# Level products of a chunked recurrence, computed and evacuated only in the columns that are queries

## What is computed

```python
def step(S, inp):
    qc, kc, vc, gc = inp
    b = jnp.cumsum(gc, axis=2)
    inter = jnp.einsum('bhtd,bhde->bhte', qc * jnp.exp(b), S)
    rel = jnp.where(lower[None, None, :, :, None],
                    b[:, :, :, None, :] - b[:, :, None, :, :], -jnp.inf)
    scores = jnp.einsum('bhtd,bhsd,bhtsd->bhts', qc, kc, jnp.exp(rel))
    intra = jnp.einsum('bhts,bhse->bhte', scores, vc)
```

## Time and profile before

| | us |
|---|---|
| median of 3 runs | 4476.14 (4475.63 to 4477.32) |
| profiled execution, time | 4479.9 |
| profiled execution, span of the trace | 4478.1 |
| TensorE busy, matmuls | 3959.1 (88%) |
| TensorE busy, weight loads | 3156.1 (70%) |
| VectorE busy | 1820.1 (41%) |
| ScalarE busy | 1096.3 (24%) |

### The profile page before, as it was taken

One profiled execution on the slowest core, in us unless ns is written; L12 is line 12 of the kernel. 1 busy time (PEld: TensorE's weight loads), 2 busy tenths in 40 slices (PEclk: granted clock), 3 DMA queues, 4 the chain that ended last, 5 costly groups with the idle time before them and its releaser, 6 DMA issues. The chain is left out here.

```text
span 4478.1 us, 55788 instructions
## 1 busy us (share of the span) xinstructions
PE 3959.1 (88%) x23797; PEld 3156.1 (70%) x23797; DVE 1820.1 (41%) x2978; ACT 1096.3 (24%) x2013; POOL 156.8 (4%) x152
## 2 busy tenths in 40 slices
PE   5798988989579999999699999999668299999996
PEld 1454455554169999999588888888644199999995
DVE  4324346752621111111278888888932611111112
ACT  1210024532110101110334554544422001010111
POOL 0000000000000000000000000000000000000000
PEclk8899988999789999999899999999889599999998
DMA  6201100013778888885310001010032478888884
GB/s 233 89 15 55 41 0 1 1 62 108 286 224 263 262 263 262 259 256 167 93 31 28 28 27 32 16 32 19 7 149 99 130 231 261 266 260 265 260 257 166
DMA packets 521950, 616.30 MB, mean 138 GB/s; under 512 B 16076, under 2 KB 466248, under 8 KB 521065
## 3 DMA queue, kind: packets, MB, share of 16 engines
q1 hardware_dynamic: 502216, 543.33, 37.3%
q0 software_dynamic: 16448, 58.73, 5.1%
q10 hardware_dynamic: 3040, 10.68, 0.6%
HBM read 558.86 MB, written 53.84 MB: 137 GB/s over the span
## 5 line engine op out<-in xcount | busy, mean ns | idle before, releaser
L1449 PEld LDWEIGHTS moe_pgu<-step_hnT,mw_w 128*128 128x128 f32 x8192 | 1118.1, 191 | 16.5 <-issue 16.5
L1449 PE MATMUL moe_pgu<-step_hnT,mw_w 128*128 128x160 f32 x8192 | 1125.8, 300 | 3.4 <-ACT step_hnT L1489 3.4
L1513 DVE TENSOR_TENSOR moe_hT<-moe_sg,moe_pgu 128x160 f32<-128x160 f32 x256 | 82.0, 321 | 1028.2 <-PE moe_pgu L1449 971.6
L1461 PE MATMUL moe_pol<-mw_w,moe_hT 128*128 128x256 f32 x2048 | 457.5, 381 | 2.3 <-DVE moe_hT L1513 1.0
L1691 PE MATMUL rec_pz<-step_hnT,rec_w 128*128 128x256 f32 x1920 | 425.2, 381 | 10.0 <-DMA rec_w<-in_r_w_in 8.0
L1461 PEld LDWEIGHTS moe_pol<-mw_w,moe_hT 128*128 128x128 f32 x2048 | 383.2, 190 | 59.0 <-DVE moe_hT L1513 10.0
L1691 PEld LDWEIGHTS rec_pz<-step_hnT,rec_w 128*128 128x128 f32 x1920 | 362.9, 191 | 58.9 <-DMA rec_w<-in_r_w_in 8.3
L1500 ACT ACTIVATE moe_sg<-moe_pgu 128x160 f32<-128x160 f32 x256 | 77.8, 304 | 1317.6 <-PE moe_pgu L1449 1317.6
L1695 PE MATMUL rec_pz<-rec_w,step_hnT 128*128 128x256 f32 x1280 | 284.8, 381 | 15.1 <-ACT rec_zg L1766 15.1
L1695 PEld LDWEIGHTS rec_pz<-rec_w,step_hnT 128*128 128x128 f32 x1280 | 241.5, 191 | 49.7 <-ACT rec_zg L1766 17.9
L1721 PE MATMUL rec_pg<-rec_ring 128*128 128x128 f32 x1600 | 198.4, 283 | 49.8 <-DVE rec_AT L2007 18.5
(11 more groups left out here) (316 smaller groups left out, 4391.6 us busy)
## 6 DMA issues: line engine op xcount, KB each, us to landing
mw_w<-in_moe_w_gu SPq DMA_DIRECT2D x256, 1024.0 KB, 11.0
mw_w<-in_moe_w_down SPq DMA_DIRECT2D x128, 1024.0 KB, 13.7
mod_w_ring<-in_mod_w SPq DMA_DIRECT2D x24, 1024.0 KB, 14.3
mw_w<-in_mod_w SPq DMA_DIRECT2D x24, 1024.0 KB, 14.3
rec_w<-in_r_w_in SPq DMA_DIRECT2D x40, 512.0 KB, 4.0
scratch_xm<-op_x ACTq DMA_DIRECT2D x20, 512.0 KB, 2.6
scratch_xn<-op_xn POOLq DMA_DIRECT2D x20, 512.0 KB, 5.2
hin_w<-in_e_w_in SPq DMA_DIRECT2D x12, 512.0 KB, 6.8
```

The source lines that it names most:

```text
L1449: m = nc.tensor.matmul(pgu[2 * (f % 2) + part][:, :], w[:, j, k, (f % 2) * P:(f % 2 + 1) * P], ring[:, k, e % 8, :], start=(k == 0), stop= ...
L1461: m = nc.tensor.matmul(pol[q // 2][:, (q % 2) * SW:(q % 2 + 1) * SW], hT[:, k, 0:CL], w[:, 8 + q, k, :], start=(k == 0), stop=(k == KD - 1))
L1513: nc.vector.tensor_tensor(hT[:, f, :], sg[:, f % 2, :], pgu[2 * (f % 2) + 1][:, :], ALU.mult).then_inc(multiplied, 1)
```

## The change

In the level products the moving operand and the output are cut to the 64 query columns of each tile; the weights stay all 128 columns. The evacuations of the levels read and write only these 64 columns, under the mask cut the same way. INTER and both DK items stay as they are. Since L64 forward no longer writes the key columns of `rec_AT`, a memset on VectorE sets these (the key half at level 64, 10 x 64 columns) to zero once a head, before VectorE waits for that product.

```diff
+        def halves(x, h, s):
+
+            return x.rearrange("p t (s h) -> p t s h", h=h)[:, :, s, :]
...
-                    into_banks(h, (d, i), lambda o, t: nc.tensor.matmul(o, kb[:, t * P:(t + 1) * P], qb[:, t * P:(t + 1) * P],
-                                                                       start=True, stop=True))
+
+                    def mm(o, t):
+                        q = qb[:, t * P:(t + 1) * P]
+                        if i != DK:
+                            q, o = (blocks(a, ITEM_LEVEL[i])[:, :, qhalf(d), :] for a in (q, o))
+                        return nc.tensor.matmul(o, kb[:, t * P:(t + 1) * P], q, start=True, stop=True)
+                    into_banks(h, (d, i), mm)
...
-                    if d == 0 and i == L64 and h:
-                        dve.wait_ge(g_full, 3 * use(h - 1, "o") + 3)
+                    if d == 0 and i == L64:
+                        if h:
+                            dve.wait_ge(g_full, 3 * use(h - 1, "o") + 3)
+                        nc.vector.memset(halves(AT[:, :, :], 64, kh), 0.0)
...
-                            last = TT(at, src, maskf[:, 0:1, :].broadcast_to([P, nt, P]), ALU.mult)
+                            last = TT(halves(at, 64, qh), halves(src, 64, qh), halves(maskf[:, 0:1, :], 64, qh).broadcast_to([P, nt, 64]), ALU.mult)
...
-                            last = nc.vector.copy_predicated(at, maskb[:, j:j + 1, :].broadcast_to([P, nt, P]), src)
+                            m = maskb[:, j:j + 1, :]
+                            if i == DK:
+                                last = nc.vector.copy_predicated(at, m.broadcast_to([P, nt, P]), src)
+                            else:
+                                hh = ITEM_LEVEL[i]
+                                m = m.rearrange("p a (b s h) -> p a b s h", s=2, h=hh)[:, :, :, qh, :].broadcast_to([P, nt, 64 // hh, hh])
+                                at, src = (x.rearrange("p t (b s h) -> p t b s h", s=2, h=hh)[:, :, :, qh, :] for x in (at, src))
+                                last = nc.vector.copy_predicated(at, m, src)
```

## The result

| | before | after |
|---|---|---|
| median, us | 4476.73 (4475.63 to 4481.53, 4 runs) | 4514.31 (4510.44 to 4515.15, 4 runs) |
| ratio after / before | | 1.0082, 95% interval 1.007 to 1.0094 |
| profiled execution, us (span) | 4479.9 (4478.1) | 4515.15 (4513.4) |

The change makes the kernel 0.8% **slower**; the forecast was 4469.2, and the range ended at 4481. Only rival D had this sign.

The account below looks back on a forecast made before the run. TensorE was taken to bound heads 0 to 6, VectorE mostly the last. Products 0, heads 0 to 6 4.1 and last head 2.8 made 6.9 us off the 4476.1 median: 4469.2 us, wanted range 4452 to 4481.

Parts of the forecast that it names:

- rival D: Halved products let TensorE's clock fall once a direction, 2.2 us each, 31 us in all, so 4500 us; chance 0.07.
- the clock of TensorE in heads 0 to 6: The sum held no clock cost in heads 0 to 6, whose windows showed a clock of 1.00.
- Products: 0: Halved level products on TensorE keep their 112 ns matmul spacing, set by the unchanged 128-column weight load; term 0.
- Rival A: Moving columns set the spacing: 112 falls to 56 ns, 63 us in heads 0 to 6, about 4406 us; chance 0.11.
- B: Spacing falls to 108 ns (4 us), or the gate copy wait shrinks (up to 15.1 us): 4450 to 4465; chance 0.24.
- Evacuations: 0.295 us a bank: VectorE's predicated copies of a bank fall from 724 to 429 ns, two-tile banks by 147 ns; about 47 us of work.
- Rival C: Evacuations out of PSUM in short runs get no shorter; only the last head's memset is left, 4476.7 us; chance 0.10.
- The memset: New VectorE memset once a head, 0.56 to 0.7 us: covered in heads 0 to 6, 0.6 us in the last.
- Heads 0 to 6: 4.1 us gained: Shorter L16 evacuation frees bank 0 0.295 us earlier, 14 times: 4.1 us off TensorE's wait and the time.
- TensorE starts L8 that much earlier, and all after it follows: In heads 0 to 6, L8 starts 0.295 us earlier per direction and the whole saving reaches the end.
- the head end "stays": TensorE's gate copy wait, 2.2 us a head, is unchanged, since both its chains hang on the DK product.
- Last head: 2.8 us gained: VectorE's work is on the path: 3 x 0.74 + 0.45 + 0.69 less 0.6 for the memset gives 2.8 us.

Follow-up runs that it names:

- e1: Changed kernel with all products computed full again, short evacuations, mask and memset kept: 4475.42 us, ratio 0.9996 to the kernel before.
- e2: Changed kernel with predicated copies over whole banks again, products halved from head 1 on, memset and short multiplication kept: 4505.26 us, ratio 1.0065.
- e5: Changed kernel with one projection product per direction moved from before L16 to between L16 and L8, products still halved: 4486.38 us, ratio 1.0017.
- e4: Changed kernel with only the L8 product halved, the other products full, evacuations short: 4480.96 us, ratio 1.0008.
- e9: Changed kernel with only the L16 product halved, the other products full, evacuations short: 4476.95 us, ratio 0.9999.
- e10: Changed kernel with only L16 and L8 halved, L64 and L32 full, evacuations short: 4509.4 us, ratio 1.0066.
- e7: Changed kernel with full products, a projection per direction moved before L8 and two last projections moved ahead of gate and norm: 4472.46 us, ratio 0.999.
- e3: Changed kernel with L64, L32 and L16 halved, the L8 product full, evacuations short: 4476.64 us, ratio 0.9998.
- e11: Changed kernel with full products, short evacuations and four added VectorE memsets ahead of the L16 evacuation, lengthening TensorE's pause: 4533.56 us, ratio 1.0124.

## Why the prediction was wrong

**The step that failed** is a term that the sum put at nothing: the clock of TensorE in heads 0 to 6. The sum has 4.1 us gained there and no price for the clock; the reason given is the sentence against rival D, answered below. The runs showed, in its place, 35.5 us for L8 and DK at the low clock and 8.5 for head ends, and with full products (e1) the 35.5 are gone.

**Products: 0. Right.** At the upper clock forty halved matmuls take 4.70 us like forty full ones (e2), and twenty take 2.34 for 2.40 us: the difference of 0.06 is the latency of the last, 219 for 275 ns, not the spacing, (2.34 - 0.22)/19 = 112 ns. Nor does the spacing shrink at the lower clock (4.50 us for twenty halved in e5's last head, 4.61 for full ones). That it is the load of 128 weight columns which keeps the pace is argued from the rows; no run changes the number of weight columns. The Trainium skill ("TensorE: Matmul & The Clock Gate", LDWEIGHTS) gives P/1.2 ns, an estimate of 107; the spacing of 112 is near it. Its isolated gap of N/2.4 + 2.5 ns (Back-to-back issue gap), by which halved products would have been worth some 60 us, does not hold here. Rival A falls, and B with it: the spacing stays at 112 ns, and the wait for the gate copy at 2.1 to 2.2 us a head.

**Evacuations: 0.295 us a bank. Right in size.** 431 ns where 429 was taken, 293 for the bank of two tiles, 419 for the multiplication. Rival C falls: runs of 8 elements out of PSUM cost no more than long ones. The memset took 0.59 us, forecast 0.56 to 0.7. TensorE's wait fell to 11.8 us in e1, forecast 11.8; with the halved products to 12.5.

**Heads 0 to 6: 4.1 us gained. Right in the wait, wrong in the time.** A smaller error is the step that let a shorter pause come straight off the end ("TensorE starts L8 that much earlier, and all after it follows"). In e1 it does follow, by 0.88 us a head, and yet four more head ends run at the low clock. The prediction took it that the head end "stays"; its wait does, but the clock behind the wait does not. It also missed the 0.28 us a head of the third wait (2 us in seven heads): what VectorE saves on the earlier levels does not all end in its own waiting.

**Last head: 2.8 us gained. Wrong.** It lost 3.0 (it takes 113.7 us before, not "some 100"). In e1, where only VectorE's part is left, it gains 1.3, with its last sixty matmuls at 9.81 us for 8.96; the halved products at the low clock cost the rest (13.14 us).

**Rival D: the mechanism that decided.** D named the clock, but had a halved product bring it down without any pause; e4 and e9 show that one halved product alone does little, and that it takes two of them around the pause. Its 31 us count from the forecast (4500); measured were 45 over the forecast. It got 0.07 for one sentence: "Against it: the halved products stand between projections and full products, in windows with a clock of 1.00." That is not so for L8. The order of work told ahead of the prediction has product L16, the buffers, evacuation L16, product L8, with no projection between, and the earlier trace rows show the pause of 1.14 us in that very place: halved product, pause, halved product. A clock of 1.00 in windows of *before* says only that full products around a pause of 1.14 us keep it up, nothing of halved ones. e10 against e9 and e4 shows that just this pair with its pause is what it takes.

The price was too small as well. 4.61 - 2.40 = 2.2 us is one product at half clock; the fall lasts over L8 and DK, mostly 3.26 us (7.96 for 4.70), in 12 directions of 14. That D's 31 us come near the 35.5 is luck: it counted all 14, and the real ones are dearer. The falls at the head ends and the last head it did not have.

The Trainium skill (same page, Part 1) says that the clock is gated by how busy TensorE has been recently, and that the monitor runs free of the program, so that the switch falls at another place from run to run. e2 agrees (4.70 and 7.96 us behind the same pause of 1.20), and so does the spread of e5, 17 us over ten runs where the kernel before spread by 9 over 31. What counts as busy the trace shows only by its effect: TensorE's busy share is above 96% in the windows at 0.94.

**What stays open.** Why e2, with the longer pause, falls in only half of the directions is not shown; that its head ends fall less often too points to where in time the pauses come, but no run separates it. Every count of falls is from one profiled execution of its kernel. e5's median is 5 us above its profiled execution; falls in more of its directions would fit that, but one profile can't show it. That the array is half idle under 64 columns is an estimate from the latencies (52 of 112 ns), not a measured quantity.

**The better version.** e7, the short evacuations with full products and the projections moved at both waits, is the fastest that was found: 4472.46 us, 0.1% below the kernel before at the edge of what can be told apart, and 42 us below the change.

## What to carry to other kernels

Going from 128 to 64 moving columns under an unchanged load of 128 weight columns gained nothing on TensorE here, and cost its clock: where two such products stand around a pause of even 1 us, look at the granted clock in windows of 1 us, not at the busy share. Before an engine's work is thinned, list for each thinned instruction what runs right ahead of it and behind it, the pauses included; that the clock is at 1.00 in the kernel before is evidence for the work before only. Time taken out of a pause comes back only if the clock in the other pauses stays as it was, so count the falls of the clock in both kernels before crediting the saving.

## What was not expected of the hardware

- A pause of 0.9 us between two products of 64 moving columns brought the clock to half in 12 of 14 places (after, e10), one of 1.2 us in 6 of 12 (e2); between full ones a pause of 1.14 us never did (before, 14 places), of 2.2 us in anything from none to all of seven head ends (none in e3 and e9, 1 before, 5 in e1, 7 in e4), of 3.5 us always (e11, 14 of 14).
- How long the low clock lasts depends on what follows: forty matmuls took 6.33 us at most when they were full (24 falls in e3, e9 and e11), and 7.60 to 7.96 in 23 of 32 falls when half of them were narrow (after, e2, e4, e10).
- With a shorter pause before L8 the falls at the head ends went from 1 to 5 of 7 (e1). e3 and e9, with the same pauses to 0.1 us, have five falls too, all before L8 and none at a head end: where the clock falls is not settled by the pause alone.
